# A ninth 2 MB slot for experts' weights, taken from the scratch area of dynamic transfers, and one more piece loaded ahead of each expert stage

## Chip, cores and metric

The kernel runs on one core of one Trainium2 chip. The metric is the device time of one execution in microseconds (us). Everything is computed in float32, or in pairs of float32r parts (a "high" and a "low" part) whose products are summed.

## The reference

Four transformer layers over 256 tokens of width 1024 run one after the other. The first two (a gated delta rule with dilated attention, then differential attention with gated linear attention, each with a convolutional feed-forward part) lie ahead of the change and are not touched. The last two have a mixer (stick-breaking attention, then retention) and a grouped mixture of 16 experts:

```
def second_block(x, c, ...):
    for i in range(DEPTH):                      # 2
        h = x * (1.0 + scale) + shift
        if i % N_MIXERS == 0:
            y = stick_breaking_attention(h, sb_w_in, sb_w_out)
        else:
            y = retention(h, positions, ret_w_in, ret_gn_g, ret_w_out)
        x = layer_norm_2(ALPHA * x + (1.0 + gate) * y, ...)
        h = x * (1.0 + scale) + shift
        y = grouped_moe(h, router_w, router_b, w_gate[i], w_up[i], w_down[i])
        x = layer_norm_2(ALPHA * x + (1.0 + gate) * y, ...)

def grouped_moe(h, ...):                        # top 2 of 16 experts for each token
    for e in range(N_EXPERTS):
        hidden = silu(t @ w_gate[e]) * (t @ w_up[e])      # 1024 -> 512
        out = out + combine[:, e:e + 1] * (hidden @ w_down[e])
```

Each of the three matrices of an expert is 1024 x 512 in float32, which is 2 MB (2,097,152 bytes). 16 experts have 48 such pieces in a layer.

## The kernel before

The program is written by hand, one instruction stream for each engine, and the streams meet at semaphores. SyncE (SP) issues nearly all weight transfers in one fixed order, the list `LOADS` that `all_loads` makes. Its stream is in order: a transfer that has to wait for its place holds up every transfer behind it.

**Slots.** A weight tile of 2 MB takes one slot of 4096 columns. Slots 0 to 2 are the tensor `ring` and serve the whole program. Slots 3 to 7 are `ringx`, one for each expert layer (`ringx0`, `ringx1`), over memory that the mixers use for other things. `WIDE` is the number of slots for experts' pieces, `EXTRA` gives the order in which an expert stage takes the slots above 2, and `ABOVE` names those that lie above the mixer's own memory and so may be filled while it still runs. `all_slots` deals the pieces over the slots in turn: piece i takes the slot that piece i - WIDE had.

**Halves.** An expert's piece is loaded in two halves of 1 MB (`load_expert`), with a semaphore for each. `load_experts` issues the pieces that are used together (mostly two: one kind of matrix for two experts) as half 0 of each, then half 1 of each. A half waits until TensorE (PE) has used the same half of the piece that had the slot before.

**Around the expert stages.** `sb_stage` is the stick-breaking attention, `ret` the retention, `moe(0)` and `moe(1)` the expert stages behind them. The projection weights of a mixer (`ws`, `wr`, `wrv`) and its output weights (`wso`, `wro`) come through slots 0 and 1. ScalarE (ACT) makes the high part of each 1024-column chunk of them (`high_half`, tile `ringhi`), VectorE (DVE) the low part (`low_half`, tile `ringlo`), and PE multiplies both. In `sb_stage` the chunks 16 to 19 are the tile `("ws", 3)`, and 20 to 27 are `wso`. Each engine walks the same list of attention units and filler work (`SBU`, `SB_FILL`), and both ACT and DVE split four chunks ahead of PE:

```
elif ...:  for kind, j, c in SB_FILL[k]:
               for _ in range(1 if kind == "T" else 4):
                   low_half(4, i)          # DVE; high_half(4, i) on ACT
                   i += 1
               if kind == "T":
                   q_tile(j, c)            # DVE takes a projected tile out of PSUM
```

So at the eighth entry of `SB_FILL` DVE does `low_half` of chunk 19, `q_tile(3, 0)`, `low_half` of chunk 20 and `q_tile(3, 1)`, in this order. PE's unit 11 takes the PSUM bank that `q_tile(3, 1)` empties.

**Experts' choice.** Only 4 experts have a fixed place; the order of the 12 others comes from the data. SP reads their numbers from the tile `eids` with 12 `value_load`s (L3408) after the first 12 pieces of a stage. There is a second round of experts for crowded inputs (8 more seats, behind a flag). In the profiled execution it is not taken, so 48 pieces are loaded in each expert stage.

Of the kernel before, what the change touches and what calls it, by code (L numbers as in the profile page):

```python
# [9 lines left out]
I32 = mybir.dt.int32  # L10
# [4 lines left out]
LAM0 = 0.8 - 0.6 * math.exp(-0.3)  # L15
LQ = math.log(128 ** -0.5)
SLOTS = 3
WIDE = 8
NEG = -1e30


# [209 lines left out]
def moe_loads(l, lo, hi):  # L231
    return [(w, l, p) for q in range(lo, hi) for w in ("mg", "mu", "md") for p in HELD[q]]


def all_loads():

    out = [("we", 6), ("we", 7), ("we", 8), ("wev",), ("wev2",)] + [("we", j) for j in range(6)]
    out += [("ada", k // 6, k % 6) for k in range(12)] + [("woe", 0), ("woe", 1)]

    def ffn(l):  # L240
        return [("wu", l, j) for j in range(11)] + [("wd", l, j) for j in range(5)] + [("wdl", l)]

    out += ffn(0)
    ada = [("ada", 2 + k // 6, k % 6) for k in range(12)]
    out += [("wo", 0), ("wo", 1), ("wo", 2), ada[0], ("wov", 0), ("wo", 3), ("wov", 1)] + ada[1:]
    out += [("woo", 0), ("woo", 1)] + ffn(1)

    one, two = moe_loads(0, 0, ALL), moe_loads(1, 0, ALL)
    out += [("ws", j) for j in (0, 4, 1, 2, 5, 3)] + one[:3] + [("wso", 0), ("wso", 1)] + one[3:]
    out += [("wr", j) for j in range(6)] + [("wrv", 0), ("wrv", 1), ("wrv", 2), ("wrv", 3), ("wr", 6), ("wr", 7)]  # L250
    out += two[:2] + [("wro", j) for j in range(4)] + two[2:]
    return out


# [2 lines left out]

EXTRA = [(5, 6, 7, 3, 4), (6, 7, 4, 5, 3)]  # L260
ABOVE = [(5, 6, 7), (6, 7)]

# [8 lines left out]
def all_slots():  # L273
# [3 lines left out]
    for name in LOADS:  # L277
# [7 lines left out]
        if name[0] in ("mg", "mu", "md"):  # L285
            k = seen[name[1]] % WIDE
            seen[name[1]] += 1
            i = EXTRA[name[1]][k] if k < WIDE - SLOTS else (turn + k - WIDE + SLOTS) % SLOTS
        else:
# [96 lines left out]
def emit(nc, ctx, ins, out):  # L386
# [5 lines left out]
    def sb(name, cols, dt=F32):  # L392
        return ctx.enter_context(nc.sbuf_tensor(name, [128, cols], dt))
# [37 lines left out]
    gate = sb("gate", 1024)  # L431
    mods = sb("mods", 96)
    lnc = sb("lnc", 128)
    small = sb("small", 640)
    posi = sb("posi", 256, I32)
    psum = ctx.enter_context(nc.psum_tensor("ps", [128, 8, 512], F32))
    scratch = nc.dram_tensor("scratch", [4, 384], F32)

# [5 lines left out]
    s_par = sem("params_landed")  # L444
    s_ring = [sem(f"ring{i}_landed") for i in range(WIDE)]
    s_more = [sem(f"second{i}_landed") for i in range(WIDE)]
    s_half = [sem(f"half{i}_landed") for i in range(4)]
    s_row, s_dec = sem("rows_landed"), sem("decay_landed")
# [3 lines left out]
    t, v, a, g, s = Lane(s_pe), Lane(s_dve), Lane(s_act), Lane(s_pool), Lane(None)  # L452
# [20 lines left out]
    xT = xTs[:, :].rearrange("p (k n) -> p k n", k=8)  # L473
    TP = TPs[:, :].rearrange("p (h n) -> p h n", h=4)
    scc = small[:, 210:218]

    adr = [tmpn[:, 0:512], tmpn[:, 512:1024]]
    scb = gate[:, 0:256].rearrange("p (k n) -> p k n", k=8)
# [129 lines left out]
    for l in range(2):  # L608
        with ExitStack() as st:
# [13 lines left out]
            M[l].pw = xTs[:, 1536:2048].rearrange("p (t n) -> p t n", t=2)  # L623
            M[l].ringx = st.enter_context(nc.sbuf_tensor(f"ringx{l}", [128, (WIDE - SLOTS) * 4096], F32))
            M[l].xh, M[l].xl = ([ap[:, h, :] for h in range(2)] for ap in (xhi, xlo))
# [957 lines left out]
    def vector():  # L1583
# [881 lines left out]
        def ret():  # L2465
# [3 lines left out]
                low_half(6, i)  # L2469

            ang, kq = Q.rtmp[0][:, 0:256], Q.rtmp[1][:, 0:256]
            ki = posi[:, :]
            c1, c2 = 6.28125, 2 * math.pi - 6.28125
            c2a = float(np.float32(np.round(c2 * 2 ** 20) / 2 ** 20))
            c2b = c2 - c2a
# [57 lines left out]
            for u, k in RETU:  # L2533
                if u is None:
                    kind, j = GATES[k]
# [51 lines left out]
    def scalar():  # L2587
# [473 lines left out]
        def ret():  # L3061
            tables("silu_and_others")
            stage_begins(5)
            a.dma_start(posi[:, :], ins["pos"].broadcast_to([128, 256])).then_inc(s_dec, 16)
            a.dma_start(Q.dec, ins["dec"]).then_inc(s_dec, 16)
            x_transposed(6, after(5), (xth, xtl), xT=Q.xT)
            for i in range(4):
# [29 lines left out]
            for u, k in RETU:  # L3097
                if u is None:
                    kind, j = GATES[k]
# [19 lines left out]
            for f in range(16):  # L3119
                high_half(6, i + f + 3)  # L3120
                if f < 2:
                    j = 8 + 4 * f
# [444 lines left out]
```

## Time and profile before

| | |
|---|---|
| time, median of 3 runs | 1760.84 us (1756.64 to 1761.62) |
| profiled execution, span from first to last instruction | 1759.8 us |
| PE busy (matmuls) | 94% of the span |
| DVE, ACT, POOL busy | 53%, 36%, 13% |
| bytes moved | 429.45 MB, mean 244 GB/s |

The profiled execution is shown by its span; no time of its own around the span is given, and the median of the runs lies 1.0 us above it. A busy PE says little here: matmuls are pipelined, and the mean hides that some stages wait for weights. "Granted clock" is the share of full speed (2.4 GHz) that the throttle gave TensorE; 0.5 is its lower level, 1.2 GHz.

### The profile page before, as it was taken

To read this page: it belongs to the slowest core of one execution; us is meant where nothing else is said; L and a number is where in the kernel's file an instruction comes from. 1 tells how busy PE (TensorE), PEld (TensorE's weight loads), DVE (VectorE), ACT (ScalarE), POOL (GpSimd) and SP (SyncE) were. 2 spreads that over 40 slices of the span, in tenths; PEclk is the share of its full clock that TensorE was granted. 3 is DMA by queue.
4 is the path that set the end of the run, shared out by engine and by line. 5 is a ranking of instruction groups with operands and counts; after the bars stand their busy time and mean duration, and the time that the engine had idled before them with its cause. 6 is when DMAs were issued, how large, how long until landed. Compare 5 with 4: busy or idle time off the path is not lost. (4 is left out here: it accounts for less than half of the span.)

```text
span 1759.8 us, 25741 instructions
## 1 busy us (share of the span) xinstructions
PE 1648.0 (94%) x10372; PEld 1226.0 (70%) x10372; DVE 937.4 (53%) x1668; ACT 627.9 (36%) x1050; POOL 228.9 (13%) x217
## 2 busy tenths in 40 slices
PE   9999998999999989999999989997789999899966
PEld 8788875699988544899888864442379898643422
DVE  1285664688642565788554766131166967732212
ACT  1035322466531224566446541110144456411101
POOL 0000000054202121263101302000000300020000
PEclk9999999999999999999999999998999999999989
DMA  8322186445553666455424766999954655699996
GB/s 328 144 96 96 66 337 268 170 166 216 192 215 122 238 275 251 162 197 193 168 96 144 301 249 260 421 421 421 390 217 144 201 225 177 259 408 421 421 420 265
DMA packets 50336, 429.45 MB, mean 244 GB/s; under 512 B 5788, under 2 KB 6048, under 8 KB 9248
## 3 DMA queue, kind: packets, MB, share of 16 engines
q1 hardware_dynamic: 47232, 417.59, 61.0%
q0 software_dynamic: 2256, 7.88, 1.3%
q10 hardware_dynamic: 720, 2.23, 0.3%
q8 instruction: 86, 1.41, 0.3%
q14 instruction: 42, 0.34, 0.1%
HBM read 426.62 MB, written 1.05 MB: 243 GB/s over the span
## 5 line engine op out<-in xcount | busy, mean ns | idle before, releaser
L88 ACT ACTIVATE arena<-ps 128x384 f32<-128x384 f32 (+5 forms) x221 | 96.4, 436 | 512.3 <-PE ps L82 305.5
L82 PE MATMUL ps<-ringx,arena 128*64 128x512 f32 (+1 forms) x1088 | 251.0, 623 | 29.6 <-DMA ring<-in_mu 19.7
L82 PE MATMUL ps<-xsplit_f,wsplit_f 128*128 128x256 f32 x2112 | 256.0, 284 | 4.2 <-ACT xsplit_f L88 2.6
L82 PEld LDWEIGHTS ps<-xsplit_f,wsplit_f 128*128 128x128 f32 x2112 | 254.1, 192 | 6.6 <-ACT xsplit_f L88 4.2
L82 PE MATMUL ps<-ring,arena 128*64 128x512 f32 (+2 forms) x768 | 238.7, 618 | 15.7 <-DMA ringx<-in_md 6.9
L91 DVE TENSOR_TENSOR wsplit_f<-ring,wsplit_f 128x1024 fp32r<-128x1024 f32 x132 | 180.2, 1369 | 70.3 <-ACT wsplit_f L88 70.3
L82 PEld LDWEIGHTS ps<-ringx,arena 128*64 128x64 f32 (+1 forms) x1088 | 75.3, 130 | 168.7 <-issue 157.7
L82 PE MATMUL ps<-xTs,ring 128*128 128x256 f32 (+1 forms) x960 | 186.0, 353 | 2.2 <-ACT xTs L88 2.2
L82 PEld LDWEIGHTS ps<-xTs,ring 128*128 128x128 f32 x960 | 161.4, 191 | 23.3 <-issue 4.8
L88 ACT ACTIVATE wsplit_f<-ring 128x1024 fp32r<-128x1024 f32 x132 | 138.1, 1051 | 57.4 <-PE ps L82 56.5
L91 DVE TENSOR_TENSOR ringlo<-ring,ringhi 128x1024 fp32r<-128x1024 f32 x88 | 120.4, 1384 | 58.6 <-ACT ringhi L88 58.3
L82 PEld LDWEIGHTS ps<-ring,arena 128*64 128x64 f32 (+2 forms) x768 | 75.8, 139 | 103.4 <-issue 97.2
L82 PE MATMUL ps<-arena 128*128 128x128 f32 (+5 forms) x1112 | 138.0, 303 | 5.7 <-DVE arena L102 2.8
L91 DVE TENSOR_TENSOR arena<-arena,ps 128x384 f32<-128x384 f32 (+1 forms) x70 | 40.7, 581 | 188.0 <-PE ps L82 182.3
L91 POOL TENSOR_TENSOR small<-small,half 128x1 f32<-128x1 f32 x16 | 9.1, 571 | 980.6 <-DVE small L95 979.0
L82 PEld LDWEIGHTS ps<-arena 128*128 128x128 f32 (+2 forms) x1112 | 123.6, 190 | 17.8 <-DVE arena L91 3.9
L99 DVE SCALAR_TENSOR_TENSOR arena<-ps,cp_sb,arena 128x255 f32<-128x255 f32 (+2 forms) x230 | 110.9, 482 | 44.0 <-ACT arena L88 32.5
L82 PE MATMUL ps<-wsplit_f,gsplit 128*128 128x512 f32 x528 | 120.1, 389 | 0.0
L82 PEld LDWEIGHTS ps<-wsplit_f,gsplit 128*128 128x128 f32 x528 | 99.0, 188 | 20.4
L88 ACT ACTIVATE ringhi<-ring 128x1024 fp32r<-128x1024 f32 x88 | 91.6, 1052 | 53.3 <-PE ps L82 44.9
L91 POOL TENSOR_TENSOR arena<-arena 128x256 f32<-128x256 f32 (+1 forms) x58 | 78.3, 1350 | 192.2 <-DVE arena L91 107.0
L82 PE MATMUL ps<-xth,ringhi 128*128 128x256 f32 x320 | 95.0, 297 | 1.9 <-DVE ringlo L91 1.4
(204 smaller groups left out, 2315.8 us busy)
## 6 DMA issues: line engine op xcount, KB each, us to landing
ring<-in_wu SPq DMA_DIRECT2D x22, 2048.0 KB, 8.5
ringx<-in_mg SPq DMA_DIRECT2D x44, 1024.0 KB, 15.5
ringx<-in_mu SPq DMA_DIRECT2D x44, 1024.0 KB, 17.9
ring<-in_ada SPq DMA_DIRECT2D x20, 2048.0 KB, 8.7
ringx<-in_md SPq DMA_DIRECT2D x32, 1024.0 KB, 17.3
ring<-in_md SPq DMA_DIRECT2D x32, 1024.0 KB, 23.7
ring<-in_wd SPq DMA_DIRECT2D x10, 2048.0 KB, 8.2
ring<-in_mg SPq DMA_DIRECT2D x20, 1024.0 KB, 15.6
```

What stands on the lines that cost most here:

```text
L82: return self.e.matmul(o, l, r, start=start, stop=stop, skip_group_check=True)
L88: return self.e.activation(o, i, f, **k)
L91: return self.e.tensor_tensor(o, a, b, op)
L99: return self.e.scalar_tensor_tensor(out=o, in0=a, scalar=s, in1=b, op0=op0, op1=op1)
```

## The change

`WIDE` goes from 8 to 9. The new slot 8 is one more 4096 columns of `ringx`, and `ABOVE` names it for both stages, so it can be filled while the mixer runs. Its room (16,384 bytes in each partition) comes from two places: the scratch area that is set aside for the descriptors of dynamic transfers shrinks to 1024 bytes, and the tile `posi` (256 columns) moves into the first 256 columns of `gate`. In `LOADS` one more expert piece stands ahead of the output weights: four instead of three ahead of `wso`, three instead of two ahead of `wro`.

```diff
-WIDE = 8
+WIDE = 9
@@ all_loads
-    out += [("ws", j) for j in (0, 4, 1, 2, 5, 3)] + one[:3] + [("wso", 0), ("wso", 1)] + one[3:]
+    out += [("ws", j) for j in (0, 4, 1, 2, 5, 3)] + one[:4] + [("wso", 0), ("wso", 1)] + one[4:]
-    out += two[:2] + [("wro", j) for j in range(4)] + two[2:]
+    out += two[:3] + [("wro", j) for j in range(4)] + two[3:]
@@
-EXTRA = [(5, 6, 7, 3, 4), (6, 7, 4, 5, 3)]
-ABOVE = [(5, 6, 7), (6, 7)]
+EXTRA = [(5, 6, 7, 8, 3, 4), (6, 7, 8, 4, 5, 3)]
+ABOVE = [(5, 6, 7, 8), (6, 7, 8)]
@@ emit
-    posi = sb("posi", 256, I32)
+    posi = gate[:, 0:256].bitcast(I32)
@@ kernel
-    nc = _bacc.Bacc("TRN2", target_bir_lowering=False, num_devices=1)
+    nc = _bacc.Bacc("TRN2", target_bir_lowering=False, num_devices=1, dynamic_dma_scratch_size=1024)
```

SP's order around the end of `sb_stage`: `ring` is slots 0 to 2, `ringx` the slots above, `in_mg`, `in_mu` and `in_md` the three kinds of expert matrices, and each row without a count is one half of 1 MB. Before:

```order
L117 DMA ringx<-in_mg 128x2048 [waits pool_done,act_done]
L117 DMA ringx<-in_mg 128x2048 x3
L117 DMA ringx<-in_mu 128x2048 x2
L117 DMA ring<-in_wso 128x2048 [waits pe_done] x4
L117 DMA ringx<-in_mu 128x2048 [waits dve_done]
L117 DMA ringx<-in_mu 128x2048
L117 DMA ringx<-in_md 128x2048
L117 DMA ring<-in_md 128x2048 [waits pe_done]
L117 DMA ringx<-in_md 128x2048
L117 DMA ring<-in_md 128x2048
L117 DMA ring<-in_mg 128x2048 [waits pe_done]
L117 DMA ring<-in_mg 128x2048 x3
```

The same place of the changed kernel, from the same row on:

```order
L117 DMA ringx<-in_mg 128x2048 [waits pool_done,act_done]
L117 DMA ringx<-in_mg 128x2048 x3
L117 DMA ringx<-in_mu 128x2048 x4
L117 DMA ring<-in_wso 128x2048 [waits pe_done] x4
L117 DMA ringx<-in_md 128x2048 [waits dve_done]
L117 DMA ringx<-in_md 128x2048 x3
L117 DMA ring<-in_mg 128x2048 [waits pe_done] x2
L117 DMA ring<-in_mg 128x2048 x2
L117 DMA ring<-in_mu 128x2048
L117 DMA ringx<-in_mu 128x2048 [waits pe_done]
L117 DMA ring<-in_mu 128x2048
L117 DMA ringx<-in_mu 128x2048 [waits pe_done]
```

Two more halves of `in_mu` now stand ahead of the four halves of `in_wso`, and behind them all of `in_md`, `in_mg` and the first half of the ninth piece (`ring<-in_mu`) come before the first transfer that waits for an expert's piece to be used. The second half of the ninth piece stands behind that transfer.

SP's order around the end of `ret`, where the second expert stage is loaded ahead. Before:

```order
L117 DMA ringx<-in_mg 128x2048 x4
L117 DMA ring<-in_wro 128x2048 [waits pe_done] x8
L117 DMA ringx<-in_mu 128x2048 [waits dve_done]
L117 DMA ringx<-in_mu 128x2048 x3
L117 DMA ringx<-in_md 128x2048 [waits pe_done]
L117 DMA ring<-in_md 128x2048
L117 DMA ringx<-in_md 128x2048
L117 DMA ring<-in_md 128x2048
L117 DMA ring<-in_mg 128x2048 x4
L117 DMA ringx<-in_mu 128x2048 [waits pe_done]
L117 DMA ringx<-in_mu 128x2048
L117 DMA ringx<-in_mu 128x2048 [waits pe_done]
```

And of the changed kernel:

```order
L117 DMA ringx<-in_mg 128x2048 x4
L117 DMA ringx<-in_mu 128x2048 x2
L117 DMA ring<-in_wro 128x2048 [waits pe_done] x8
L117 DMA ringx<-in_mu 128x2048 [waits dve_done]
L117 DMA ringx<-in_mu 128x2048
L117 DMA ringx<-in_md 128x2048
L117 DMA ringx<-in_md 128x2048 [waits pe_done]
L117 DMA ringx<-in_md 128x2048 x2
L117 DMA ring<-in_mg 128x2048 x4
L117 DMA ring<-in_mu 128x2048
L117 DMA ringx<-in_mu 128x2048 [waits pe_done]
L117 DMA ring<-in_mu 128x2048
```

Here two halves of `in_mu` moved ahead of `in_wro`, and again one single half of the ninth piece (`ring<-in_mu`) stands ahead of the transfer that waits for an expert's piece to be used.

## Rows read from the trace of the kernel before

**Rows 1.** The page's span; issue to landing of 1 MB transfers that mostly run alone.

```profile
span 1759.8 us, 25741 instructions
...
ring<-in_ws SPq DMA_DIRECT2D x12, 1024.0 KB, 5.1
```

**Rows 2.** Stretches of moe(0): us, busy PE, PEld, DVE, ACT, POOL, clock, DMA, GB/s.

```profile
1080.00:1100.00 20.00, 19.03 (x96) 6.93 (x94) 7.16 (x21) 2.80 (x6) 9.37 (x4) 1.00 1.02 424
...
1240.00:1260.00 20.00, 12.50 (x112) 3.73 (x108) 2.80 (x4) 1.79 (x3) 0.00 (x0) 1.00 1.01 420
```

**Rows 3.** SP's transfers by time, in moe(0), then in moe(1): start, us.

```profile
1071.08 4.24 SPq L117 DMA_DIRECT2D ringx<-in_mu  x4
1078.81 4.24 SPq L117 DMA_DIRECT2D ringx<-in_md  x4
1090.04 0.36 SPq L117 DMA_DIRECT2D ringx<-in_mg  x1
...
1539.57 4.24 SPq L117 DMA_DIRECT2D ringx<-in_mu  x4
...
1558.64 0.36 SPq L117 DMA_DIRECT2D ringx<-in_mg  x1
```

**Rows 4.** Median us to landing of transfers issued at 1090.0, 1248, 1558.6 and 1718.5.

```profile
ringx<-in_mg SPq DMA_DIRECT2D x1, 1024.0 KB, 6.9
...
ring<-in_md SPq DMA_DIRECT2D x2, 1024.0 KB, 24.6
...
ringx<-in_mg SPq DMA_DIRECT2D x1, 1024.0 KB, 6.5
...
ring<-in_md SPq DMA_DIRECT2D x2, 1024.0 KB, 22.7
```

**Rows 5.** Line L3408, the reads of experts' numbers on SP: ns min/median/max, first and last start.

```profile
L3408 SPq TENSOR_LOAD <-eids x24: 261/261/478, 1083.1 to 1557.6; - x24
```

**Rows 6.** SP's transfers at the end of sb_stage, and wso's first half issue to landing.

```profile
975.49 2.33 SPq L117 DMA_DIRECT2D ringx<-in_mg  x4
977.86 0.97 SPq L117 DMA_DIRECT2D ringx<-in_mu  x2
984.13 24.95 SPq L117 DMA_DIRECT2D ring<-in_wso  x4
...
ring<-in_wso SPq DMA_DIRECT2D x1, 1024.0 KB, 14.7
```

**Rows 7.** ACT, DVE and PE in order of time, behind that landing.

```profile
998.83 2.00 ACT L88 ACTIVATE ringhi<-ring 128x1024 fp32r<-128x1024 f32 x2 [3.66 <-DMA ring<-in_wso]
...
999.92 1.23 DVE L91 TENSOR_TENSOR ringlo<-ring,ringhi 128x1024 fp32r<-128x1024 f32 x1 [0.95 <-ACT ringhi L88]
1001.26 0.42 DVE L95 TENSOR_SCALAR arena<-ps 128x256 f32<-128x256 f32 x1
...
1001.74 0.86 PE L82 MATMUL ps<-arena 128*64 128x256 f32 x4 [0.84 <-DVE arena L95]
```

**Rows 8.** Issue to landing: POOL's row loads (issued 996-997) and wso's second half (990.2).

```profile
lnp<-in_rows POOLq DMA_DIRECT2D x2, 512.0 KB, 6.7
...
ring<-in_wso SPq DMA_DIRECT2D x1, 1024.0 KB, 11.6
```

**Rows 9.** As rows 2: matmuls at half and full clock; PE's longest stall, the stretch behind.

```profile
1062.00:1065.00 3.00, 3.00 (x15) 2.77 (x14) 2.69 (x14) 0.00 (x0) 0.00 (x0) 0.51 0.00 0
1065.00:1067.00 2.00, 2.00 (x19) 2.00 (x19) 1.93 (x9) 0.90 (x2) 0.00 (x0) 1.00 0.00 0
...
1682.97 1.07 PE L82 MATMUL ps<-ringx,arena 128*32 128x512 f32 x3 [6.19 <-DMA ring<-in_mu]
...
1683.00:1686.00 3.00, 3.00 (x16) 0.84 (x20) 0.00 (x0) 0.00 (x0) 0.00 (x0) 0.50 1.01 421
```

**Rows 10.** wro's first half (issued 1435.75) to landing, and ACT's first chunk of it.

```profile
ring<-in_wro SPq DMA_DIRECT2D x1, 1024.0 KB, 8.1
...
1459.86 1.05 ACT L88 ACTIVATE ringhi<-ring 128x1024 fp32r<-128x1024 f32 x1
```

More of the change, by code:

```diff
@@ L2471, in ret @@
             ang, kq = Q.rtmp[0][:, 0:256], Q.rtmp[1][:, 0:256]
-            ki = posi[:, :]
+            ki = posi
             c1, c2 = 6.28125, 2 * math.pi - 6.28125
@@ L3063, in ret @@
             stage_begins(5)
-            a.dma_start(posi[:, :], ins["pos"].broadcast_to([128, 256])).then_inc(s_dec, 16)
+            a.dma_start(posi, ins["pos"].broadcast_to([128, 256])).then_inc(s_dec, 16)
             a.dma_start(Q.dec, ins["dec"]).then_inc(s_dec, 16)
```

## The prediction, made before the changed kernel ran

> **What bounds the kernel now.** I read the stretches first. In both expert stages the DMA engines move 420 to 424 GB/s at a share of 1.01 to 1.02, whether PE is busy (19.03 of 20 us) or idle a third of the time (12.50 of 20) [rows 2]. So from the first refill of a slot to the last landing a stage lasts as long as its bytes do. At 421 GB/s a half of 1 MB (1.0486 MB) takes 2.49 us, a piece 4.98. A stage has 96 halves. 16 are issued before the first refill, at 1071.08 and 1539.57 [rows 3]. The other 80 take 199 us. The sum closes: with about 2.9 us before the first data (a lone transfer needs 5.1 from issue to landing, 2.49 of it data [rows 1]) the last lands at 1273 and 1741.5, and 1248 + 24.6 and 1718.5 + 22.7 [rows 4] give 1272.6 and 1741.2. PE's later waits, the 6.19 us one among them [rows 9], are for such landings.
>
> Then I read SP's own order in time, since a ninth slot acts through it, and then ACT, DVE and PE around the one place where the added transfers push others back.
>
> **The changed order in the expert stages.** The ninth slot sounds like 4.98 us less for each stage. SP's order gives half of it. Pieces come in pairs, half 0 of both and then half 1 of both. With 8 slots both members of a pair take the slots of one earlier pair. With 9 the first member takes the second slot of the pair before, the other one waits for an expert's piece to be used. So ahead of the first refill stand 17 halves instead of 16: the order shows one `ring<-in_mu`, then the waiting transfer, and the ninth piece's other half behind it. 79 halves are left: -2.49 us.
>
> A part of that is lost again a few microseconds later. SP issues 8 halves from 1071.08 to 1083.05, then reads 12 expert numbers (L3408, from 1083.1 [rows 5]) and issues the next half only at 1090.04 [rows 3], where it lands 6.9 later, at 1096.9 [rows 4]. In the changed order only 7 halves are to be had in that time (the eighth went ahead). They land from 1076.3 on at 2.49 each, the last at 1091.2. The next one can't land before 1090.04 + 5.1 to 5.4 = 1095.3, since SP is still reading. The DMA engines idle 1.6 us, and the stage gains 1096.9 - 1095.3 = **1.6 us**. In moe(1) the half issued at 1558.64 lands 6.5 later, at 1565.1 [rows 3, 4]. There SP has one transfer less to issue before it reads, and the half no longer waits for a piece in use, so I put its issue at 1557.9 and its landing at 1563.2: **1.9 us**. Both are bounded above by 2.49 and below by about 1.0, if an issue with an address from a register takes longer to start. Behind this point transfers are issued 9 us and more ahead of their data, and one slot more only adds to that, so no other gap opens. Everything behind the last landing moves with it. Sum: **-3.5 us** (-2.0 to -5.0).
>
> **The output weights of sb_stage.** This is where I expect the loss. SP issues mg x4 and mu x2 from 975.49 to 978.83 and wso's first half at 984.13, which lands 14.7 later, at 998.8 [rows 6]: a lone one needs 5.1 [rows 1], the rest is the queue in front. ACT waits 3.66 us for just this landing and starts at 998.83. DVE's low part of that chunk starts at 999.92, 0.95 of idle before it, behind it stands the `q_tile` at 1001.26, and at 1001.74 PE's unit 11 starts 0.06 us after that ends, having waited 0.84 [rows 7]. So landing, ACT, DVE, PE is a chain without slack already. The changed order puts two more halves in front of wso: **+4.98 us** on it.
>
> Behind DVE's waiting instruction stand four units' outputs (`oT`) and two more low parts. PE's tile_splits of chunks 18 and 19 wait for banks which those outputs free, and the last four attention units wait for the tiles that come of them. PE goes through all of it in order, so nothing absorbs the delay: down_split, the norm, moe(0)'s router and the first refill all come later by it. What was hidden and what is late next is therefore the same thing, the whole rest of the program.
>
> Two additions. POOL's two row loads are issued at 996 to 997 and land 6.7 later, while wso's second half lands at 990.2 + 11.6 = 1001.8, 3.0 behind the first instead of 2.49 [rows 8]: 0.5 us for the part of the 1 MB of rows that passed. Before, the first half had landed ahead of them; now all of them pass in front of it: **+1.0 us** (0.5 to 2.5, where 2.5 is 1 MB at 421 GB/s). By the Trainium skill (DMA: Bandwidth & Descriptors, Queues, rings and completion order) each DMA engine goes round robin between queues at packet granularity. By that rule POOL's whole 1 MB is served before wso's half, and if bandwidth simply adds up the term would be the upper bound; the row of before shows 0.5 for a part of it, and the measured side gets more weight.
>
> And the clock: PE now stands still for 0.84 + 6.0 = 6.8 us. Behind its longest stall, 6.19 us, PE ran 3 us at 0.50 granted clock, the 1.2 GHz level. At half clock 15 matmuls go in 3 us, at full clock 19 in 2 us [rows 9]. So in 3.3 us at half clock 16.5 matmuls are done instead of 31, and the rest takes 1.5 us: **+1.5 us** (0 to 3.3, if it stays low twice as long). The work there is dense (48 split matmuls), so it feels it. Sum for sb_stage: **+7.5 us** (5.0 to 10.8).
>
> **The same push in ret is free.** wro's first half lands 8.1 after 1435.75, at 1443.9, and ACT takes its first chunk at 1459.86 [rows 10]. Two more halves in front make it 1448.9: 11 us of cover are left. If that cover were gone, it would cost up to 5 us.
>
> **Moved at no cost.** `posi` in `gate` has the same DMA and the same casts, long before `gate` is filled again. The two pieces of the next stage that SP issues once moe(0) has landed wait for one more slot's bookkeeping, 0.1 to 0.3 us, under the norm. Nothing is added on PE, ACT, DVE or POOL.
>
> **Sum.** -3.5 + 7.5 = +4.0 us on a span of 1759.8, that is 1763.8, and with the 1.0 us by which the median of the runs lies above it, **1764.8 us**. 0.3% (5.3 us) is what a measurement of this kernel can tell from no change, so this is "same" by a narrow margin. Both halves of the sum are larger than the result.
>
> **Rivals.**
> Hidden after all: wso's lateness is absorbed, for instance because it lands earlier than I say. Then only the gain is left, 1757.3, at the full 2.49 for each stage 1755.8. This decides when wso lands no later than before; each us of lateness takes 1 us, and from 3.5 us on the change loses. For it speaks only that ACT, two instructions on, sits idle anyway. Against it: DVE is the one that matters, and waited already. Chance 0.10.
> Heavier: the row loads pass at full price (2.5) and the clock stays low twice as long (3.3), with stages gaining 3.0: 5.0 + 2.5 + 3.3 - 3.0 = +7.8, 1768.6. This is the other side of my forecast, slower in measure. The step over the bound needs only 1.3 us more than my sum. Chance 0.17. (By the round-robin rule of the Trainium skill named above, the price of the row loads is this full one.)
> POOL waits for room: the scratch area is 1/16 of what it was, and POOL could hold each row load until the one before it has landed, 5.1 to 6.7 us [rows 8]. The Trainium skill (SBUF — State Buffer, SBUF size: 192, 224, or 256?) says that this area is the ring for descriptors of software transfers and has 16 KiB. POOL issues at most two transfers together and its rows are needed a whole stage later, so this costs nothing; at worst the one early transfer through `scratch` costs 5 us once, 1769.8. Chance 0.03.
> The slot does what its name says: 4.98 for each stage, with wso late as forecast: -10 + 7.5, 1758.3. SP's order is against it. Chance 0.03.
> My forecast, net +1.5 (no additions, 1762.3) to +6: 0.67.
>
> **Numbers.** The range that leaves out 2 in 10 is 1757.5 to 1769. Slower by over 0.3% (above 1766.1): the upper part of the forecast, 0.14, most of "heavier", 0.14, and POOL's, 0.02: 0.30. Faster by over 0.3% (below 1755.6) needs the hidden case and full gains and some luck: 0.05. Same: 0.65.
>
> **What would show it.** wso's first half landing 19.5 to 21 us after issue instead of 14.7; ACT's wait for it 8.5 to 10 us instead of 3.66; PE's wait for DVE's `q_tile` 6 to 7 us instead of 0.84, with the clock at 0.5 for some us; the first refill of moe(0) at 1077 to 1080 instead of 1071.08. From there 79 halves to the last landing, with one gap of 1 to 2 us where the expert numbers are read. In moe(1) the first refill, counted from moe(0)'s last landing, unchanged, and the last landing 1.5 to 2.5 us earlier relative to it. I am wrong if wso's lateness doesn't reach PE, if sb_stage loses more than 9 us, or if a stage gains more than 2.5.

## The result, and the profile after

The changed kernel takes 1769.36 us (median of 6 runs, 1767.78 to 1772.28), the kernel before 1761.93 in the same comparison: ratio 1.0047, 95% interval 1.0032 to 1.0061. (The quotient of the two medians is 1.0042, inside the interval.) It is slower by more than the 0.3% named as the bound. The forecast was 1764.8, with a range up to 1769.0.

The mean granted clock of the six runs was 0.975, 0.976, 0.976, 0.975, 0.978 and 0.974. The page of the changed kernel gives its span. That execution took 1772.28 us, 1.8 more than its span.

```profile
span 1770.5 us, 25745 instructions
```

**wso comes late, and everything behind it.** First the issue-to-landing view, for the transfer that SP issues at 989.07 (wso's first half), for the one at 995.16 (its second) and for POOL's rows. They answer to 14.7, 11.6 and 6.7 us in [rows 6, 8].

```profile
ring<-in_wso SPq DMA_DIRECT2D x1, 1024.0 KB, 21.5
...
ring<-in_wso SPq DMA_DIRECT2D x1, 1024.0 KB, 18.7
...
lnp<-in_rows POOLq DMA_DIRECT2D x2, 512.0 KB, 11.2
```

Then ACT, DVE and PE in order of time, the same four instructions as in [rows 7]:

```profile
1010.64 2.00 ACT L88 ACTIVATE ringhi<-ring 128x1024 fp32r<-128x1024 f32 x2 [10.52 <-DMA ring<-in_wso]
1011.73 1.22 DVE L91 TENSOR_TENSOR ringlo<-ring,ringhi 128x1024 fp32r<-128x1024 f32 x1 [7.82 <-ACT ringhi L88]
1013.06 0.42 DVE L95 TENSOR_SCALAR arena<-ps 128x256 f32<-128x256 f32 x1
1013.54 0.69 PE L82 MATMUL ps<-arena 128*64 128x256 f32 x1 [7.70 <-DVE arena L95]
```

Three numbers grew together: the landing comes 6.8 us later after issue, ACT's wait is 10.52 instead of 3.66, PE's wait 7.70 instead of 0.84. From the landing (1010.6) to PE's matmul it is 2.9 us, as before (998.8 to 1001.74). The delay goes through one for one.

POOL's rows were issued at 1001.27 and 1001.89 and landed at 1010.87 and 1014.63, both behind wso's first half. Between 1005 and 1011 us the two queues moved, as packets, MB and share of the DMA engines (SP's queue first, then POOL's):

```profile
q1 hardware_dynamic: 214, 1.61, 65.6%
q0 software_dynamic: 213, 0.81, 34.2%
```

As many packets went from one as from the other, and the rows' packets are 4 KB where the weights' are 8 KB, so the rows got a third of the bytes: 0.81 MB of their 1.05 by 1011 us.

The stretches behind it (columns as in [rows 2]) show the clock. PE does nothing for 7.6 us, then 21 matmuls in 5.20 us at 0.50, then 49 in 5.60 at 0.99. The kernel before did the same first matmuls at full clock, and the changed one falls 2.15 us further behind it while the clock is low; at its later stop shown below it is still 2.1. The last row is a stretch from 8 to 5 us ahead of the first refill. About there (9 to 6 us ahead) the kernel before stood at 0.51 for 3 us, the first stretch of [rows 9]; here the clock is full.

```profile
1005.90:1013.50 7.60, 0.00 (x0) 0.00 (x0) 1.65 (x2) 2.00 (x2) 0.00 (x0) 0.67 1.02 413
1013.50:1018.70 5.20, 5.16 (x21) 4.44 (x22) 4.60 (x9) 0.00 (x0) 0.00 (x0) 0.50 0.14 59
1018.70:1024.30 5.60, 5.58 (x49) 5.22 (x48) 1.23 (x1) 2.43 (x5) 0.00 (x0) 0.99 0.14 22
...
1075.90:1078.90 3.00, 2.82 (x24) 2.75 (x24) 2.69 (x14) 0.10 (x1) 0.00 (x0) 1.00 0.00 0
```

PE's last stop of over 1.5 us ahead of that refill, in the changed kernel and then in the kernel before, is the mark up to which the time behind the wait is measured below:

```profile
1073.33 0.62 PE L82 MATMUL ps<-arena,kc_sb 128*128 128x16 f32 x4 [1.58 <-DVE arena L91]
```

```profile
1059.39 0.62 PE L82 MATMUL ps<-arena,kc_sb 128*128 128x16 f32 x4 [1.59 <-DVE arena L91]
```

**The expert stages gain 1.2 and 1.4 us here** (1.5 and 1.6 in the mean of the four profiles of each kernel below). SP's transfers of moe(0) in order of time; beside [rows 3], seven halves instead of eight stand ahead of the read of the experts' numbers, and the next is issued at 1102.29:

```profile
1083.78 0.33 SPq L117 DMA_DIRECT2D ringx<-in_mu  x1
...
1087.59 7.68 SPq L117 DMA_DIRECT2D ringx<-in_md  x4
1102.29 2.40 SPq L117 DMA_DIRECT2D ringx<-in_mg  x4
```

Their issue-to-landing times: the seventh half (issued 1094.94), the next one (1102.29), and the last of the stage (1259.28), which answers to 24.6 in [rows 4].

```profile
ringx<-in_md SPq DMA_DIRECT2D x1, 1024.0 KB, 9.1
...
ringx<-in_mg SPq DMA_DIRECT2D x1, 1024.0 KB, 4.9
...
ringx<-in_md SPq DMA_DIRECT2D x1, 1024.0 KB, 26.1
```

The seventh lands at 1104.0, the next at 1107.2: 3.1 us apart instead of 2.49, and the one behind it another 3.4: 1.5 us without data. The kernel before had one such gap at this place, also 3.1 between landings, so 0.6 of the 1.5 was lost before as well. In a window around the gap the DMA engines' share falls from 1.01 to 0.90. In moe(1) the window that also holds POOL's rows stands at 0.94:

```profile
1100.00:1104.10 4.10, 4.10 (x22) 1.38 (x20) 0.76 (x1) 0.60 (x1) 4.02 (x3) 1.00 0.90 328
...
1570.00:1580.00 10.00, 10.00 (x50) 3.41 (x48) 5.69 (x19) 1.20 (x2) 4.19 (x4) 1.00 0.94 369
```

**ret doesn't wait.** wro's first half (issued 1447.65) lands 12.8 later, at 1460.4, and ACT takes its first chunk at 1471.76: 11.3 us of cover.

```profile
ring<-in_wro SPq DMA_DIRECT2D x1, 1024.0 KB, 12.8
...
1471.76 1.05 ACT L88 ACTIVATE ringhi<-ring 128x1024 fp32r<-128x1024 f32 x1
```

**And 4.9 us that I had not forecast.** The last ws transfer is issued at 979.99 instead of 975.05, before anything that was moved. Most of it arises near 77 us: SP's transfers stand 0.6 us behind those of the kernel before at 66 us, 5.3 at 159 and 4.9 at 975. First the window of the changed kernel, then the same window of the kernel before:

```profile
76.70:90.30 13.60, 13.60 (x43) 10.02 (x43) 7.60 (x20) 2.19 (x9) 0.00 (x0) 0.50 0.29 125
```

```profile
76.70:90.30 13.60, 13.01 (x66) 10.45 (x66) 9.73 (x24) 3.30 (x12) 0.00 (x0) 1.00 0.25 105
```

43 matmuls instead of 66, all of them at half clock. Whether this belongs to the change or to chance was the first question for the runs.

### The profile page after: what moved, and what is told of

Same layout as the page of the kernel before. It is cut to its first block and busy times, and to the rows that moved or that the text cites. A ratio compares the mean times of both kernels' runs of the same rounds, so it can differ in the third digit from the quotient of the medians.

```text
span 1770.5 us, 25745 instructions
## 1 busy us (share of the span) xinstructions
PE 1652.0 (93%) x10372; PEld 1226.5 (69%) x10372; DVE 937.0 (53%) x1668; ACT 628.3 (35%) x1050; POOL 228.0 (13%) x217
## 3 DMA queue, kind: packets, MB, share of 16 engines
HBM read 426.62 MB, written 1.05 MB: 242 GB/s over the span
## 5 line engine op out<-in xcount | busy, mean ns | idle before, releaser
L82 PE MATMUL ps<-ring,arena 128*32 128x512 f32 (+2 forms) x736 | 210.6, 627 | 33.4 <-DMA ringx<-in_mu 20.3
L82 PEld LDWEIGHTS ps<-ring,arena 128*32 128x32 f32 (+2 forms) x736 | 69.7, 140 | 147.5 <-issue 132.3
```

Source lines behind the costliest of these rows:

```text
L82: return self.e.matmul(o, l, r, start=start, stop=stop, skip_group_check=True)
```

## The experiments

Theory: the loss is wso's place behind two more halves, and no more than that; the room costs nothing. Rivals: the room (moved addresses, the smaller scratch area) costs time early on; or contention with POOL's rows, or the clock as a threshold, makes most of the loss. Each comparison ran beside the kernel before, whose medians were 1762.30 us (first four), 1760.63 (next four) and 1762.49 (first8, lazy8).

All runs are told by the same measures from their traces, in us: "sb_stage" is from SP's issue of the last ws transfer to the first refill of moe(0), "moe" from the first refill to the last landing, "ret" what lies between the two expert stages.

**Room alone.** The kernel before with 8 slots, and of the change only this:

```diff
-    posi = sb("posi", 256, I32)
+    posi = gate[:, 0:256].bitcast(I32)
...
-    nc = _bacc.Bacc("TRN2", target_bir_lowering=False, num_devices=1)
+    nc = _bacc.Bacc("TRN2", target_bir_lowering=False, num_devices=1, dynamic_dma_scratch_size=1024)
```

> The kernel before with 8 slots, of which only the room is changed as in the ninth-slot version: the scratch area of dynamic transfers is 1024 bytes, and `posi` lies in `gate`. No transfer is moved. Theory (wso's lateness is the loss, the room is free): ratio 1.000, within 0.1%, 1760 to 1763 us; SP's transfer at 975 us of the kernel before stands within 0.5 us of there, unless a low clock falls into the first 100 us. Rival (the room itself, through moved addresses or the smaller area, brings the part that the three terms of the ninth-slot version leave open, 4.9 us before 975 us in its profile and 1.6 to 2 us of its median): ratio 1.001 to 1.003, 1763.5 to 1767 us, with PE behind within the first 100 us and the granted clock at 0.5 for some 14 us near 77 us again.

Measured: 1761.47 us, ratio 0.9995 (0.9984 to 1.0007), sb_stage 95.93 (before 96.03), last ws transfer at 974.84, 0.5 clock for 3.4 us near 77. The room costs at most 1.2 us by the interval.

**Ninth slot, three pieces ahead of wso as before.**

```diff
-    ... + one[:4] + [("wso", 0), ("wso", 1)] + one[4:]
+    ... + one[:3] + [("wso", 0), ("wso", 1)] + one[3:]
```

> The ninth slot is kept with everything that belongs to it, but only three pieces of the experts' weights stand ahead of wso in SP's order, as before; the fourth follows wso. Theory: wso's first half lands 14.7 us after its issue again, PE waits 0.8 us for DVE's q_tile instead of 7.7, the clock stays at full speed there, and sb_stage loses nothing. The two gains of the expert stages (1.2 and 1.4 us) stay: about 2.5 us under the time before, 1759.4 us, ratio 0.9986 (0.9975 to 1.000). Rival (the room costs 2 us and more early on, or the loss in sb_stage comes from the contention with POOL's row loads rather than from the place in SP's order): 1761 to 1765 us, not under the time before.

Measured: 1759.60, ratio 0.9988 (0.9978 to 0.9998); sb_stage 95.99, moe(0) 201.87, moe(1) 201.55. Its ACT and PE, in order of time, wait as in the kernel before:

```profile
999.35 2.01 ACT L88 ACTIVATE ringhi<-ring 128x1024 fp32r<-128x1024 f32 x2 [3.59 <-DMA ring<-in_wso]
...
1002.25 0.86 PE L82 MATMUL ps<-arena 128*64 128x256 f32 x4 [0.77 <-DVE arena L95]
```

With one list index changed back the loss is gone and the gain stays. The time forecast (1759.4) was met.

**Ninth slot, wso ahead of all expert pieces** (`[("wso", 0), ("wso", 1)] + one`).

> The ninth slot is kept, and wso stands ahead of all expert pieces. Theory: wso lands some 15 us before ACT wants it, so that its wait of 3.66 us and PE's of 0.84 go as well; sb_stage is 0.8 us shorter than before (3.6 at most if ACT's wait was the bound and not DVE's), the rest as in the version with three pieces ahead: 1758.6 us, ratio 0.998 (0.9965 to 0.9995). The expert pieces of moe(0) are issued 5 us later than with three ahead, but all 17 halves still land before the first refill. Rival (something else of sb_stage is as late as wso, so that nothing is won beyond before): the same time as with three pieces ahead. Second rival (pieces that land later make PE wait at the start of moe(0)): 1761 us and more.

Measured: 1756.56, ratio 0.9972 (0.9961 to 0.9983), under the forecast 1758.6; sb_stage 93.81. wso lands 4.9 us after issue, as a lone transfer does, and PE's only wait at that place is for POOL:

```profile
ring<-in_wso SPq DMA_DIRECT2D x1, 1024.0 KB, 4.9
...
999.90 1.19 PE L82 MATMUL ps<-arena 128*64 128x256 f32 x8 [0.26 <-POOL arena L3247]
...
1060.00:1063.00 3.00, 2.82 (x22) 2.46 (x21) 2.69 (x14) 0.00 (x0) 0.00 (x0) 1.00 0.00 0
```

sb_stage is 2.2 us shorter than before, more than the 0.84 us wait. The last row says where most of the rest is: ahead of the first refill the clock is full, where the kernel before had 0.51 [rows 9], and the matmuls there take 1.2 us less.

**POOL's rows moved.** The changed kernel with four pieces ahead, but the rows for this stage are loaded behind its attention units:

```diff
-            elif n != 5:
+            elif n not in (4, 5):
                 load_rows(n)
...
+            load_rows(4)
             norm(4)
```

> The ninth-slot version as it is, with four pieces ahead of wso, but POOL loads its rows of layer norm weights for the stage behind the attention units of sb_stage, not beside wso's landing. It tells the price of 1 MB of row loads in a full queue from that of the two halves. Theory (the two measured deltas of wso's halves, 2.95 and 3.75 us, hold 1.9 us of row loads): wso's first half lands 19.6 instead of 21.5 us after its issue, PE's wait falls from 7.7 to about 6, and the time from 1769.4 to 1767.5, ratio to before 1.003 (1.002 to 1.0045). Rival A (the rows are served in full, as if bandwidths added): 2.5 us less, 1766.9. Rival B (they only share the time in which wso waits anyway, and the bound is elsewhere): no change, 1769.4.

Measured: 1767.08, ratio 1.0035 (1.0020 to 1.0050), sb_stage 101.36. Issue to landing of wso's halves, and ACT and PE behind the first:

```profile
ring<-in_wso SPq DMA_DIRECT2D x1, 1024.0 KB, 19.7
...
ring<-in_wso SPq DMA_DIRECT2D x1, 1024.0 KB, 16.1
...
1003.35 2.00 ACT L88 ACTIVATE ringhi<-ring 128x1024 fp32r<-128x1024 f32 x2 [8.67 <-DMA ring<-in_wso]
...
1006.25 0.69 PE L82 MATMUL ps<-arena 128*64 128x256 f32 x1 [5.85 <-DVE arena L95]
```

This is the cleanest split of the delay. Two halves alone: 19.7 - 14.7 = 5.0 us. The rows on top: 21.5 - 19.7 = 1.8 for the first half, and 18.7 - 16.1 = 2.6 by the second, which is all of the 1 MB at 2.49. (In the four profiles of the changed kernel the landings are 21.2 to 21.5 and 18.5 to 18.7, so 1.5 to 1.8 and 2.4 to 2.6.) The time came near the forecast 1767.5.

**Changed kernel again.**

> The changed kernel once more, for more runs and a second profile. The three terms read from its first profile (7.8 us lost in sb_stage, 1.2 and 1.4 gained in the expert stages) come to +5.2 us, 1767.5 beside 1762.3 for the kernel before, ratio 1.0030; its first six runs gave 1769.4, and its first profile had 4.9 us more before 975 us with a granted clock of 0.5 for 13.65 us near 77 us. Theory (the early low clock comes by chance, in either kernel): the second profile shows it shorter or not at all, SP's transfer at 979.99 us stands at 974 to 977, the span is 1764 to 1766, and the ratio over all runs is 1.003 to 1.004. Rival (it belongs to the changed kernel): it is there again, and the median is 1769 once more.

Measured: 1766.49 (6 runs), ratio 1.0042 (1.0025 to 1.0058), span 1764.5. No low clock near 77 us, last ws transfer at 974.77, sb_stage 103.72, moe 201.82 and 201.59. So the median came near the 1767.5 of the three terms, and the ratio stayed above their 1.0030 (the quotient of the medians is 1.0033).

**Half the push.** Only half 0 of the fourth piece ahead of wso:

```diff
-                    load_expert(name, src(name), h)
+                    if (name, h) != (("mu", 0, 4), 1):
+                        load_expert(name, src(name), h)
...
+                if name == ("wso", 1):
+                    load_expert(("mu", 0, 4), source(("mu", 0, 4)), 1)
```

> Half the push: of the fourth expert piece only half 0 stands ahead of wso in SP's order, half 1 right behind wso. All else is the changed kernel's. Theory (each 1 MB half ahead of wso delays ACT, DVE and PE one for one, and the row loads of POOL come on top in part): wso's first half lands 17.2 to 18.5 us after its issue, PE's wait for DVE's q_tile is 3.4 to 4.5 us (0.84 before, 7.70 in the changed kernel), sb_stage loses 3 to 4.5 us and the whole stands at +0.5 to +2 us, 1763 to 1764.5, ratio 1.0008 (0.9998 to 1.0018). Rival (a threshold: the clock or a missed turn makes most of the loss at once): either no loss in sb_stage, ratio 0.9988, or nearly all of it, 1.003 and more.

Measured: 1763.15, ratio 1.0017 (1.0008 to 1.0027), sb_stage 100.40. The landing, PE's wait, and the stretch at half clock around it:

```profile
ring<-in_wso SPq DMA_DIRECT2D x1, 1024.0 KB, 17.4
...
1002.75 0.69 PE L82 MATMUL ps<-arena 128*64 128x256 f32 x1 [3.58 <-DVE arena L95]
...
1001.90:1008.60 6.70, 5.85 (x24) 5.13 (x25) 5.29 (x11) 0.00 (x0) 0.00 (x0) 0.50 0.48 196
```

One half is 2.7 us of landing (2.49 are its own bytes) and 2.7 of PE's wait, two halves were 6.8 with the rows: the delay is a dose, not a threshold. sb_stage lost 4.4, though, 1.6 more than the wait. In this trace the clock is at 0.5 for 6.8 us behind the wait and for 6.8 once more ahead of the router, where the kernel before has 3.4 and 3.4. The loss by the clock doesn't follow the length of the wait. With a wait of 5.85 us (the run with POOL's rows moved) it was at 0.5 for 6.8 us at the wait and for 3.4 some 14 us behind it.

**Expert numbers read one pair at a time**, on top of wso first and nine slots:

```diff
-                    for j in range(16):
-                        if j not in FIXED:
+                    for j in HELD[q]:
+                        if j not in FIXED and j not in fresh:
```

> Ninth slot, wso ahead of all expert pieces, and SP reads an expert's number only ahead of the first transfer that needs it, instead of all 12 in a row. Theory (what the ninth slot lost against its 2.49 us per stage is the gap in the queue while SP reads for 6.5 to 7.3 us): no landing behind the first refill is more than 2.6 us after the one before it in that place, moe(0) takes 200.3 us from first refill to last landing instead of 201.7, moe(1) 200.8 instead of 201.6 (POOL's rows stay), together 2 to 3 us less than with wso first alone: 1754 us, ratio 0.9957 (0.9945 to 0.997). Rival (a transfer with an address from a register starts late by itself, whatever SP did before): the gap of 3.1 to 3.4 us stays, and the time is that of wso first, 1756.6.

Measured: 1754.73, ratio 0.9962 (0.9948 to 0.9977); moe(0) 200.24, moe(1) 200.82. SP issues the next half at 1084.77, 1.9 us behind the seventh and not 7.3, and the DMA engines stand at their full share over the 20 us that follow:

```profile
1084.77 7.84 SPq L117 DMA_DIRECT2D ringx<-in_mg  x4
...
1085.00:1105.00 20.00, 19.98 (x94) 6.81 (x96) 6.46 (x20) 2.16 (x5) 8.29 (x4) 1.00 1.01 420
```

Both stage lengths came as forecast to 0.1 us, and the 3.1 and 3.4 us between landings are gone. The gap was SP's read, not a late start of a transfer with an address from a register. With the kernel that follows it is the fastest of those tried, 5.9 us under the kernel before; against wso first alone the gain rests on the stage lengths, since the two intervals of the ratios overlap.

**The whole ninth piece ahead.** As the last, and the pair in which the ninth slot falls is issued piece by piece:

```diff
-            for h in range(2):
-                for name in names:
-                    load_expert(name, src(name), h)
+            order = [(name, h) for h in range(2) for name in names]
+            if names[0] == ("mu", names[0][1], 8):
+                order = [(name, h) for name in names for h in range(2)]
+            for name, h in order:
+                load_expert(name, src(name), h)
```

> As the one before, and the two pieces among which the ninth slot falls are issued piece by piece (both halves of the first, then both of the second), so that the whole ninth piece stands ahead of the first refill: 18 halves instead of 17. Theory (a stage lasts as long as the halves that are left behind the first refill, 2.49 us each): 78 are left, moe(0) and moe(1) take 2.49 us less each, the time is 5 us less than with the reads spread alone: 1749 us, ratio 0.993 (0.9915 to 0.9945). Rival (the first refill then comes later, or PE waits for the half that now comes behind): 1752 to 1755.

Measured: 1754.36, ratio 0.9965 (0.9953 to 0.9977): a miss. moe(0) 199.98 and moe(1) 199.75 us, 0.3 and 1.1 shorter instead of 2.5 each. The rival was right that something eats it, and right on the time (it had 1752 to 1755), though not on what: the first refill comes 93.8 us behind the last ws transfer in both. The first refill brings one half now, and the next slots come free 3.4 and 3.9 us apart:

```profile
1071.36 3.76 SPq L117 DMA_DIRECT2D ringx<-in_mu  x2
...
1076.00:1087.00 11.00, 10.03 (x54) 3.92 (x52) 4.13 (x16) 1.60 (x4) 3.40 (x2) 1.00 0.93 366
```

One half is 2.49 us of work for the DMA engines and the next piece in use is released 3.4 us later, so they run dry twice (landings 3.05 and 3.72 us apart): 1.8 us of idling in place of the half that went ahead (1.5 in moe(1), at 2.9 and 3.6). The pace at which PE gives slots back bounds this stretch, not the bytes.

**wso first with 8 slots** (the kernel before, `[("wso", 0), ("wso", 1)] + one`).

> The kernel before, 8 slots and its own room, only with wso ahead of all expert pieces. It tells what the place of wso is worth without the ninth slot. Theory: sb_stage is 2.2 us shorter (93.8 instead of 96.0 us from the last ws transfer to the first refill, as in the three profiles with wso first), the expert stages keep 202.8 to 203.1 us; 2.2 us under the time before, ratio 0.9988 (0.998 to 0.9998). With nine slots and wso first the ratio was 0.9972, so the ninth slot would be worth 2.6 us. Rival (wso first only pays together with the ninth slot): ratio 1.000. Beside it, for the early low clock: with the room of the kernel before, a stretch at 0.5 near 77 us in this profile or the one below would show that the changed room has no part in it.

Measured: 1760.43, ratio 0.9996 (0.9985 to 1.0007); sb_stage 95.24. A miss by the profile: 0.8 us, the size of PE's wait, instead of 2.2. The time can't decide it: the medians are 2.1 us apart, and the interval holds nothing as well as the forecast 0.9988. Its stretch ahead of the first refill has the half clock that the versions with nine slots and wso first don't show:

```profile
1058.30:1061.60 3.30, 3.25 (x14) 2.93 (x14) 2.99 (x16) 0.00 (x0) 0.00 (x0) 0.50 0.00 0
```

**Spread reads with 8 slots.**

> The kernel before, 8 slots, SP reads an expert's number only ahead of the first transfer that needs it. Theory (with 8 slots eight halves are in the queue when SP reads, so only 0.6 and some 0.1 us were lost): moe(0) takes 202.2 us instead of 202.8, moe(1) 202.3 to 202.9, ratio 0.9995 (0.999 to 1.0003). So the read is worth little with eight slots and 2.3 us with nine. Rival (the reads are worth as much without the ninth slot): 1.5 us and more per stage, ratio 0.998.

Measured: 1762.47, ratio 1.0005 (0.9996 to 1.0014); moe(0) 202.78, moe(1) 202.97 (before 202.83 and 202.93). Nothing that can be told from none with eight slots (a miss in moe(0), where 202.2 was expected), 1.4 and 0.9 us with nine. And near 77 us, in a program which is the kernel before up to the expert stage:

```profile
76.00:86.20 10.20, 10.20 (x32) 7.38 (x31) 6.45 (x18) 1.98 (x8) 0.00 (x0) 0.50 0.27 113
```

**More profiles of both kernels.**

> The kernel before once more, for a second profile: is there a stretch at 0.5 granted clock near 77 us, as there was in five of nine profiles with the changed room (13.65, 3.41, 3.41, 10.24 and 10.24 us) and not in the first profile of before? Theory (chance, in either kernel): about one profile in two has it; where it is there, the last ws transfer comes at 977 to 980 instead of 974 to 975. Rival (the room brings it): never with the room of before.

> A third profile of the changed kernel. Theory (the rest is the granted clock: behind a wait of 7.7 us it can stay low longer, and it can fall again near the router, than the two profiles at hand show): sb_stage takes 103.7 to 106 us from the last ws transfer to the first refill, the expert stages 201.6 to 201.8 us each, ret 264 to 267 us; where sb_stage is longer than 103.8, it has more microseconds at 0.5. Rival (the rest comes of chance outside sb_stage, near 77 us and in ret, in either kernel alike): sb_stage stands at 103.7 to 103.8 again.

> A fourth profile of the changed kernel, expected as the third.

> A third profile of the kernel before. Both theories: sb_stage 96.0 to 96.1 us, as in two profiles of it and in three kernels that have wso's place unchanged; expert stages 202.8 to 203.3 us; ret 263 to 266 us; the last ws transfer at 974 to 976, or later with a stretch at 0.5 near 77 us.

> A fourth profile of the kernel before, expected as the third.

Measured, with the two profiles at hand (us; "last ws" is when SP issues it, "low near 77" the time at 0.5 there):

```
          span    last ws  low near 77  sb_stage  moe(0)  ret     moe(1)
before    1759.8  975.05   0            96.03     202.83  265.66  202.93
before    1758.9  974.68   0            96.09     203.25  264.34  203.24
before    1761.4  976.14   3.4          96.04     202.99  265.58  203.32
before    1764.3  979.77   13.7         96.17     203.42  264.82  202.87
mean      1761.1  976.41                96.08     203.12  265.10  203.09
after     1770.5  979.99   13.7         103.79    201.63  266.04  201.56
after     1764.5  974.77   0            103.72    201.82  265.23  201.59
after     1760.9  972.40   0            103.30    201.60  264.79  201.52
after     1769.3  979.14   13.7         103.55    201.56  266.16  201.43
mean      1766.3  976.58                103.59    201.65  265.56  201.53
```

The fourth profile of the kernel before has the early stretch as the first of the changed one had it:

```profile
76.50:90.10 13.60, 13.60 (x43) 10.12 (x43) 7.42 (x20) 2.19 (x9) 0.00 (x0) 0.50 0.29 123
```

So the early low clock comes and goes in either kernel, and where it lasts 13.7 us it moves everything behind it by some 4 us. The theory that the rest was made in sb_stage fell: its length hardly varies (103.3 to 103.8), and neither do the expert stages. What varies is the part before 975 us, by 7.6 us between profiles of one kernel, and a little ret. The means differ by 5.2 us: +7.5 in sb_stage, -1.5 and -1.6 in the expert stages, +0.5 in ret, +0.2 before 975 us, +0.1 at the end.

## Why the prediction was wrong, step by step

**wso's place (+7.5): right, and the size too, though its parts were not.** Landing, ACT, DVE and PE moved as one chain, nothing absorbed it, and sb_stage lost 7.5 us in the mean of four profiles. The two halves cost 5.0 (forecast 4.98). The rows cost 1.5 to 1.8, not 1.0: the trace of before showed 0.5 for a part of them, and I gave it more weight than the upper bound. Nor was it the full 2.5 at the first half. The Trainium skill (DMA: Bandwidth & Descriptors, Queues, rings and completion order) has each DMA engine go round robin between queues packet by packet. The trace agrees: 213 packets of one queue went beside 214 of the other. My step from there, that the whole 1 MB is served before wso's half, did not follow. The rows' packets are half as large, both rows landed behind the first half, and only the 0.8 MB that had passed until then delayed it (1.9 us at 421 GB/s, an estimate); the full price (2.4 to 2.6 us) shows by the second half, which PE did not wait for. The clock took 2.1 us (1.5 forecast), because it stayed low for 5.2 us behind the wait and not for 3.3: from PE's start at 1013.54 to the end of its last stop of over 1.5 us ahead of the refill, at 1073.33, it is 59.8 us, and was 57.7 before. It gave 1.2 back behind that stop (10.4 us to the refill instead of 11.7), where its low stretch is missing, which I had not forecast: 0.9 net. Two errors, of up to 0.8 and of 0.6 us, cancelled, so it is partly luck that the sum was met.

**The expert stages (-3.5): the mechanism right, the size too large.** 17 halves ahead, 79 left, a gap where SP reads: all seen, and the run with spread reads shows the read to be its cause. The gains were 1.5 and 1.6 (forecast 1.6 and 1.9). In moe(0) the DMA engines had no data for 1.5 us at the read (forecast 1.6), spread over two landings. In moe(1) the half behind the read landed 1.9 us earlier as forecast, and three halves on, with POOL's rows in the queue, 0.6 of it went in the first profile (landings 3.9 apart instead of 3.4). Together 3.0, not 3.5.

**ret (0): its weights are covered, 11.3 us are left (11 forecast).** But ret is longer by 0.5 us in the mean. With 263.3 to 267.4 us over all runs this can't be told from chance.

**The sum, and the step that failed.** None of the three signs of being wrong came: wso's lateness reached PE, sb_stage lost under 9 us, no stage gained over 2.5. The three terms that the change moves were forecast at +4.0 and measured at +4.5 in the mean of the profiles. The step that failed is the last one: "-3.5 + 7.5 = +4.0 us on a span of 1759.8, and with the 1.0 us by which the median of the runs lies above it", with a range added up from the bounds of those terms alone. It takes one profile and three runs for the kernel and puts everything outside the moved places at nothing. The runs showed in its place: the part before 975 us alone differs by 7.6 us between executions of the changed kernel, by 5.1 of the kernel before, and the spans by 9.6 and 5.4. The measured median lies 4.6 us above the forecast. 1.1 of that is the base: the kernel before had 1761.93 in the comparison, not 1760.84. The other 3.4 are the change itself, +7.4 by the medians: 0.5 for the gains that were too large, 0.7 in parts that the change doesn't touch (with them +5.2 in all by the profiles, ratio 1.0030), and 2.2 that the profiles don't show as a term.

**What stays open.** The two comparisons gave 1.0047 and 1.0042, 1.2 to 1.7 parts in a thousand above the 1.0030 of the profiles (2 to 3 us). The lower ends of both intervals hold it nearly (1.0032) and fully (1.0025). All 14 executions of the changed kernel on record have a mean of 1768.5 us and all 80 of the kernel before 1762.0: +6.5, give or take some 1.5 (an estimate from their scatter), which holds the profiles' 5.2. So the second comparison and the whole record leave room for the profiles' sum, and the first barely does.

A part of the first six runs' excess goes with their clock. Each 0.001 of mean granted clock less goes with 1.2 us more in the changed kernel's executions and 1.0 in those of the kernel before. Its profiles with the 13.7 us near 77 had 0.974 and 0.975, those without 0.979 and 0.980; five of the first six runs had 0.976 or less, two of the second six. The first six had 0.9757 in the mean, the four profiles 0.9768, worth 1.3 us. That is a link read off the numbers; no run changed the clock alone to show it. Nor is it shown that the early low clock is equally frequent in both kernels: 8 of 14 executions of the changed one had 0.976 or less, while of the kernel before, whose clock is 0.001 higher without it, 12 of 71 had 0.977 or less. The room alone doesn't bring it (none of its 12 runs was at 0.977 or less, and it costs 1.2 us at most); whether chance or something else in the changed kernel does stayed untested. Why the low stretch ahead of the router is there or not (there with 8 slots and wso first, not with 9) was not found either.

**The rivals.** "Hidden after all" fell with the first trace. "Heavier" named 1768.6, close to the measured time, but not by its mechanism: the rows cost 1.5 to 1.8 at the half that counts and not 2.5, the clock 0.9 net and not 3.3, and only the gains of 3.0 were as it said. "POOL waits for room" cost nothing: POOL issues its two row loads 0.6 us apart, and the room alone is at 0.9995. "The slot does what its name says" is wrong in this order, and the run with the whole piece ahead shows that the order isn't all: the stages gain 2.9 and 3.2 us there, with 1.8 us lost where slots come free too slowly.

## What to carry to other kernels

Another slot in a saturated queue is worth no more than what goes out before the first refill, less every gap that the fuller queue had covered: look for the place where the issuing engine does something else, and for the pace at which slots come free. Count each transfer put ahead in the same queue as a delay of its full length at the landing (5.0 us for two halves here), bytes of another queue by what passes until that landing (0.8 of 1.05 MB here), and follow the landing through to the engine that waits; here one list index made the difference between 1.0047 and 0.9988, and taking the urgent weights first made it 0.9972. And before summing microseconds on one profile, ask how much the same kernel varies ahead of the change: here by 5.1 and 7.6 us, more than the effect that was forecast, and the range has to hold it.

## What the runs showed of the hardware

- The granted clock stood at 0.5 for 13.7, 10.2, 3.4 or 0 us near 77 us in executions whose instructions are the same up to there, with no stop of PE over 1.3 us in the 70 us before. 43 matmuls instead of 66 went in 13.6 us, and the rest of the program moved by some 4 to 5 us.
- In the changed kernel, with its wait of over 7 us, the clock was at 0.5 for 10.2 us in three profiles and for 6.8 in one, part of it within the wait; with a wait of 5.85 us for 6.8 and 14 us later for 3.4; with a wait of 3.6 us for 6.8; in the kernel before, with 0.84 us, for 3.4 some 12 us later. Where the wait was over 5 us, or gone with nine slots, the low stretch ahead of the first refill was missing, 1.2 us less; where it was 3.6 us, that stretch was twice as long. With wso first and eight slots, no wait, both low stretches were there as in the kernel before. These are one to four profiles of each case.
- 1 MB from POOL's queue beside a full SP queue delayed the transfer beside which it passed by 1.5 to 1.8 us and the next by 2.4 to 2.6. The two queues took turns by the packet (214 and 213 between 1005 and 1011 us), 8 KB against 4 KB, and shared one rate: 405 GB/s in that window, 421 for SP's queue alone [rows 2].
- SP took 7.3 us from one issue over twelve reads of numbers to the next issue, some 0.54 us for each number, of which the load is 0.26 [rows 5]; 5.4 us of it went away where it read them one pair at a time, and the rest hid under transfers already in the queue.
